# Peer lookup of a two-block layer: bank order of an output product, a choice cut in pieces, scores moved behind their queries

## The reference

```python
def peer(h, w_query, sub_keys, expert_down, expert_up):
    qry = (ht @ w_query).reshape(T, PEER_HEADS, 2, PEER_HALF)
    sub_scores = jnp.einsum('thpc,hpkc->thpk', qry, sub_keys)
    top_s, top_i = lax.top_k(sub_scores, K)
    cand_s = top_s[:, :, 0, :, None] + top_s[:, :, 1, None, :]
    cand_id = top_i[:, :, 0, :, None] * N_KEYS + top_i[:, :, 1, None, :]
    best_s, best_c = lax.top_k(cand_s.reshape(T, PEER_HEADS, K * K), K)
    expert_id = jnp.take_along_axis(cand_id..., best_c, axis=-1)
    gate = jax.nn.softmax(best_s, axis=-1)
    ...
        u = expert_down[ib]
        a = jnp.einsum('pd,ped->pe', xb, u)
        act = jax.nn.gelu(a, approximate=False) * gb
        v = expert_up[ib]
        return jnp.einsum('pe,ped->pd', act, v)
```

## Time and profile before

| | us |
|---|---|
| median of 3 runs | 1179.24 |
| lowest and highest run | 1175.29, 1180.07 |
| profiled execution | 1178.07 |
| its span | 1176.3 |
| PE busy | 1030.6 (88%) |
| DVE busy | 855.7 (73%) |
| ACT busy | 419.9 (36%) |
| POOL busy | 285.8 (24%) |
| DMA, mean over the span | 322 GB/s |
| mean granted clock of TensorE | 0.956 |

### The profile page before, as it was taken

How to read it: one execution, slowest core, us unless ns; L and a number is a source line. 1 busy time by engine, 2 the same in 40 slices (tenths; PEclk the granted TensorE clock), 3 DMA queues, 4 the chain that set the end, 5 groups by cost and what they waited for, 6 DMA issues and landing times.

```text
span 1176.3 us, 14387 instructions
## 1 busy us (share of the span) xinstructions
PE 1030.6 (88%) x5156; PEld 721.4 (61%) x5156; DVE 855.7 (73%) x1780; ACT 419.9 (36%) x833; POOL 285.8 (24%) x260
## 2 busy tenths in 40 slices
PE   6999999999999999988899998888668767887878
PEld 6988999999998876874555544333323323332433
DVE  5977689998868993384778767766786677677554
ACT  5644544445456654233223222221221222222112
POOL 0000000000000000034445543454335434443520
PEclk9999999999999999989999998898899889888998
DMA  9532449979927433479999999999999999999994
GB/s 357 204 125 90 147 180 350 354 293 322 326 89 309 139 109 124 180 284 340 364 420 422 422 421 421 422 420 421 423 422 421 422 422 419 423 421 421 422 421 183
DMA packets 67896, 378.61 MB, mean 322 GB/s; under 512 B 7537, under 2 KB 7921, under 8 KB 35057
## 3 DMA queue, kind: packets, MB, share of 16 engines
q0 software_dynamic: 36864, 268.45, 55.3%
q1 hardware_dynamic: 29808, 106.09, 25.0%
q10 hardware_dynamic: 1152, 3.15, 0.8%
HBM read 376.61 MB, written 1.05 MB: 321 GB/s over the span
## 4 chain that ended last, share of the span: by engine, by line
PE 45%; DMA 31%; DVE 15%; ACT 5%; issue 4%; POOL 1%; SPq 0%; DVEq 0%; ACTq 0%
DMA whi_rows<-in_peer,idsb 26%; PE pb L905 7%; PE pb L428 7%; PE pb L425 7%; PE pb L908 6%; PE pb L453 4%; DMA ring_sb<-in_peer,idsb 3%; DVE ring_lo L1417 3%; PE pb L640 2%; PE pb L810 2%; PE pb L860 1%; DVE ring_sb L2006 1%; PE pb L470 1%; PE pb L472 1%; PE pb L471 1%
## 5 line engine op out<-in xcount | busy, mean ns | idle before, releaser
L2006 DVE CUSTOM_DVE_ANT_0 ring_sb<-ring_sb,arena 128x1024 f32<-128x1024 f32 x137 | 166.9, 1225 | 106.8 <-DMA ring_sb<-in_peer,idsb 106.8
L905 PE MATMUL pb<-ring_sb,arena 128*128 128x512 f32 x274 | 154.2, 646 | 98.8 <-ACT arena L1358 98.7
L2062 POOL DMA_INDIRECT ring_sb<-in_peer,idsb x137 | 150.4, 1098 | 237.0 <-PE pb L908 210.2
L425 PE MATMUL pb<-xhi,whi 128*128 128x256 f32 x736 | 190.9, 293 | 1.1 <-ACT xhi L986 0.5
L428 PE MATMUL pb<-xlo,whi 128*128 128x256 f32 x736 | 186.3, 287 | 0.5 <-DVE xlo L1636 0.3
L2062 POOL DMA_INDIRECT arena<-in_peer,idsb x38 | 41.4, 1090 | 546.2 <-DVE idsb L1984 503.4
L1353 ACT ACTIVATE arena<-arena 128x4 f32<-128x4 f32 (+2 forms) x71 | 14.6, 205 | 400.4 <-DVE arena L2006 400.4
L1417 DVE TENSOR_TENSOR ring_lo<-ring_sb,whi 128x1024 fp32r<-128x1024 f32 x126 | 147.6, 1218 | 13.4 <-ACT whi L959 13.3
L905 PEld LDWEIGHTS pb<-ring_sb,arena 128*128 128x128 f32 x274 | 52.3, 202 | 167.9 <-issue 167.4
L908 PE MATMUL pb<-ring_sb,arena 128*128 128x512 f32 x274 | 151.0, 634 | 0.0
L425 PEld LDWEIGHTS pb<-xhi,whi 128*128 128x128 f32 x736 | 142.5, 194 | 5.4 <-issue 3.4
(11 more groups left out here) (356 smaller groups left out, 1783.8 us busy)
## 6 DMA issues: line engine op xcount, KB each, us to landing
ring_sb<-in_ada SPq DMA_DIRECT2D x48, 512.0 KB, 5.6
ring_sb<-in_w_gu SPq DMA_DIRECT2D x44, 512.0 KB, 6.9
ring_sb<-in_w_in SPq DMA_DIRECT2D x38, 512.0 KB, 8.3
ring_sb<-in_w_down SPq DMA_DIRECT2D x22, 512.0 KB, 5.9
ring_sb<-in_w_out SPq DMA_DIRECT2D x16, 512.0 KB, 3.6
ring_sb<-in_w_q SPq DMA_DIRECT2D x8, 512.0 KB, 3.6
whi_rows<-in_w_q SPq DMA_DIRECT2D x6, 512.0 KB, 7.5
ring_sb<-in_peer,idsb POOLq DMA_INDIRECT x137, 27.7
```

What stands on the lines that cost most here:

```text
L425: e.matmul(o, hi_w(u)[:, c], xh(k), start=start, stop=False, skip_group_check=skip)
L905: mm = e.matmul(pb[4 + 2 * tile][:, :], dgr[col % 8], o[:, 1024:1536], start=begin, stop=end)
L2006: e.tensor_tensor_reduce(o, o, h2t[tile], 1.0, 0.0, MUL, ADD, aa[:, col:col + 1]).then_inc(*VD.up(("dot", col)))
L2062: e.indirect_dma_start(rows_at[s], None, peer, bass.IndirectOffsetOnAxis(ap=idsb[:, col:col + 1], axis=0)).then_inc(s_row[s], 16)
```

## The change

1. The output product's four banks are taken one at a time, each just before its first use, in the order 0, 2, 3, 1 counted from the next in turn.
2. `experts` is cut into `best_of_list`, `pair_up`, `best_of_pairs` and `decode`, and `prepare` into `dot` and `weigh`. DVE's second choice (n = 1) stands in pieces between the dot products of rows 0 to 3. ACT's exponential of that choice moves behind group 1's scaled identities.
3. PE's query for tile 0 of head 2 moves behind the products of group 0; `second_sums` moves one group later. On ACT the root of tile 1's norm moves ahead of group 2's GELU.
4. The queries of heads 3 to 7 come one group earlier, and behind the products of that point instead of ahead of them; head 2's tile 1 moves from group 5 to group 9. Scores follow their queries by two groups, and ACT copies queries and scores one and three groups behind. Choice 3 moves from group 8 to 9, choices 4 to 15 one group later each.
5. POOL's table `after` counts from GR[i - 1]: buffers of heads 0 and 1 enter the list four rows later, head 2's twenty rows later, those of heads 3 to 7 behind the same row as before.

```diff
@@ -363,9 +363,9 @@
-        second_at = {3: 0, 4: 1, 5: 2}
-        query_at = {6: (3, 0), 7: (3, 1)} | {4 * h - 8 + j: (h, j) for h in range(4, 8) for j in range(2)}
-        choose_at = {4: 2, 8: 3} | {4 * n - 6: n for n in range(4, 16)}
+        second_at = {3: 0, 4: 1, 9: 2}
+        query_at = {5: (3, 0), 6: (3, 1)} | {4 * h - 9 + j: (h, j) for h in range(4, 8) for j in range(2)}
+        choose_at = {4: 2, 9: 3} | {4 * n - 5: n for n in range(4, 16)}
@@ -817,9 +817,10 @@
-            outs = [bank((VN, ("wo2", 2 * i + 1, 0))) for i in range(4)]
-            where["wo2"] = outs
+            outs = where["wo2"] = [(turn[0] + i) % 4 for i in (0, 2, 3, 1)]
+            turn[0] += 4
             for i in range(4):
+                bank((VN, ("wo2", 2 * i + 1, 0)), outs[i])
                 out_half(0, i, range(4, 8), pb[outs[i]])
             for i in range(4):
                 out_half(0, i, range(4), pb[outs[i]])
@@ -916,7 +917,6 @@
-            query_tile(2, 0)
@@ -926,21 +926,23 @@
             for i in range(NB + 1):
-                if i in second_at:
-                    query_tile(second_at[i], 1)
-                if i in query_at:
-                    query_half(*query_at[i])
                 if i == 60:
                     keep_clock(10)
                 if i:
                     add_rows(i - 1)
                 if i == 1:
+                    query_tile(2, 0)
+                if i == 2:
                     second_sums()
                     scores(2, (0,))
+                if i - 2 in second_at:
+                    scores(second_at[i - 2], (1,))
+                if i - 2 in query_at and query_at[i - 2][1]:
+                    scores(query_at[i - 2][0], (0, 1))
                 if i in second_at:
-                    scores(second_at[i], (1,))
-                if i in query_at and query_at[i][1]:
-                    scores(query_at[i][0], (0, 1))
+                    query_tile(second_at[i], 1)
+                if i in query_at:
+                    query_half(*query_at[i])
@@ -1320,15 +1322,17 @@
             def query_tile(h, tile):
                 e.wait_ge(*(USED.at(U_wq[2 * h + 1]) if tile else PQ.at(("qry", h))))
                 if h == 2:
-                    e.wait_ge(*PQ.at(("SC", 0, tile)))
+                    e.wait_ge(*PQ.at(("SC", 4) if tile else ("SC", 0, 0)))
...
             def query(h):
                 e.wait_ge(*USED.at(U_wq[2 * h + 1]))
-                e.wait_ge(*PQ.at(("SC", h - 2) if h >= 5 else ("SC", h - 2, 1)))
                 if h == 4:
                     e.wait_ge(*PQ.at(("SC", 2, 0)))
+                    e.wait_ge(*PQ.at(("SC", 0, 1)))
+                else:
+                    e.wait_ge(*PQ.at({3: ("SC", 1, 1), 5: ("SC", 3), 6: ("SC", 2, 1), 7: ("SC", 5)}[h]))
                 e.activation(qry[h % 2], pb[where["qry", h]][:, :], ACT.Copy).then_inc(*AQ.up(("qry", h)))
@@ -1370,27 +1374,28 @@
             choose(0)
             second_gate(range(4))
-            choose(1)
-            second_gate(range(4, 8))
             for i in range(NB + 1):
-                if i - 1 in query_at and query_at[i - 1][1]:
-                    scores(query_at[i - 1][0], (0, 1))
-                if i - 1 in second_at:
-                    scores(second_at[i - 1], (1,))
+                if i == 2:
+                    n3_root(1)
                 if i < NB:
                     prepare(i)
                 if i == 0:
+                    second_gate(range(4, 8))
+                if i == 1:
+                    choose(1)
                     query_tile(2, 0)
                     second_squares()
-                if i == 1:
-                    n3_root(1)
+                if i == 2:
                     scores(2, (0,))
-                if i == 2:
                     shifted(1)
-                if i in second_at:
-                    query_tile(second_at[i], 1)
-                if i in query_at and query_at[i][1]:
-                    query(query_at[i][0])
+                if i - 3 in second_at:
+                    scores(second_at[i - 3], (1,))
+                if i - 3 in query_at and query_at[i - 3][1]:
+                    scores(query_at[i - 3][0], (0, 1))
+                if i - 1 in second_at:
+                    query_tile(second_at[i - 1], 1)
+                if i - 1 in query_at and query_at[i - 1][1]:
+                    query(query_at[i - 1][0])
                 if i in choose_at:
                     choose(choose_at[i])
@@ -1923,32 +1928,44 @@
-            def experts(n):
+            def best_of_list(n, p):
...
+            def pair_up(n):
...
+            def best_of_pairs(n):
                 e.wait_ge(*VT.at((n, "cand")))
+                e.wait_ge(*AE.at(n - 1))
+                top16(cand, cand2, bsv, bcu[:, :], n, "best")
+                e.wait_ge(*VT.at((n, "best", "index2")))
+                e.tensor_scalar(nb, bsv[:, 0:1], -1.0, None, MUL).then_inc(*VT.up((n, "nb")))
+
+            def experts(n):
+                best_of_list(n, 0)
+                best_of_list(n, 1)
+                pair_up(n)
                 if n:
-                    e.wait_ge(*AE.at(n - 1))
-                    top16(cand, cand2, bsv, bcu[:, :], n, "best")
-                    e.wait_ge(*VT.at((n, "best", "index2")))
-                    e.tensor_scalar(nb, bsv[:, 0:1], -1.0, None, MUL).then_inc(*VT.up((n, "nb")))
+                    best_of_pairs(n)
                     decode(n, 0, 16)
                     return
@@ -1994,21 +2011,26 @@
+            def dot(col):
...
+            def weigh(i):
...
+            def prepare(i):
+                for col in GR[i]:
+                    dot(col)
+                weigh(i)
@@ -2027,12 +2049,22 @@
             choose(0)
-            choose(1)
-            for i in range(NB + 1):
+            best_of_list(1, 0)
+            dot(0)
+            best_of_list(1, 1)
+            dot(1)
+            pair_up(1)
+            weigh(0)
+            best_of_pairs(1)
+            dot(2)
+            dot(3)
+            decode(1, 0, 16)
+            weigh(1)
+            second_add()
+            gates(1)
+            for i in range(2, NB + 1):
                 if i < NB:
                     prepare(i)
-                if i == 0:
-                    second_add()
                 if i == 2:
                     second_norm()
@@ -2047,7 +2079,7 @@
-            after = {GR[i - 2][-1]: h for i, h in second_at.items()} | {GR[i - 2][-1]: h for i, (h, j) in query_at.items() if j}
+            after = {GR[i - 1][-1]: h for i, h in second_at.items()} | {GR[i - 1][-1]: h for i, (h, j) in query_at.items() if j}
```

More of the change, by code:

```diff
@@ L1924, in top16 @@
                 e.max_index(idx[:, 8:16], vals[:, 8:16], tmp_).then_inc(*VT.up((*name, "index2")))
-            def experts(n):
+            def best_of_list(n, p):
                 tile, h = n // 8, n % 8
-                if n == 0:
-                    e.wait_ge(*PQ.at(("SC", 0, 0)))
-                elif tile == 0:
-                    e.wait_ge(*AQ.at(("SC", h) if h >= 3 else ("SC", h, 0)))
-                if n:
-                    e.wait_ge(*VT.at((n - 1, "gates")))
-                    e.wait_ge(*VTI.at(n - 1))
-                for p in range(2):
-                    s = SC[tile][:, (2 * h + p) * 128:(2 * h + p + 1) * 128] if n else pb[where["SC", h, 0]][:, p * 128:(p + 1) * 128]
-                    if p:
-                        e.wait_ge(*VT.at((n, 0, "index2")))
-                    top16(s, sc2[:, 0:128], tsv[:, p * 16:p * 16 + 16], tiu[:, p * 16:p * 16 + 16], n, p)
+                if p == 0:
+                    if n == 0:
+                        e.wait_ge(*PQ.at(("SC", 0, 0)))
+                    elif tile == 0:
+                        e.wait_ge(*AQ.at(("SC", h) if h >= 3 else ("SC", h, 0)))
+                    if n:
+                        e.wait_ge(*VT.at((n - 1, "gates")))
+                        e.wait_ge(*VTI.at(n - 1))
+                s = SC[tile][:, (2 * h + p) * 128:(2 * h + p + 1) * 128] if n else pb[where["SC", h, 0]][:, p * 128:(p + 1) * 128]
+                if p:
+                    e.wait_ge(*VT.at((n, 0, "index2")))
+                top16(s, sc2[:, 0:128], tsv[:, p * 16:p * 16 + 16], tiu[:, p * 16:p * 16 + 16], n, p)
+            def pair_up(n):
                 e.wait_ge(*VT.at((n, 1, "index2")))
@@ L1995, in choose @@
                 gates(n)
-            def prepare(i):
-                for col in GR[i]:
-                    tile = col // 128
-                    s, v = row_of[col]
-                    o = rows_at[s][:, 0:1024]
-                    e.wait_ge(s_row[s], v)
-                    if col % 128 == 0:
-                        for g in range(2):
-                            e.wait_ge(*AQ.at((("h2t", tile), g)))
-                    e.tensor_tensor_reduce(o, o, h2t[tile], 1.0, 0.0, MUL, ADD,
-                                           aa[:, col:col + 1]).then_inc(*VD.up(("dot", col)))
+            def dot(col):
+                tile = col // 128
+                s, v = row_of[col]
```

(7 more changed lines are left out.)

1 line of the change is left out of this document (added).

## The result

| | before | after |
|---|---|---|
| median | 1178.90 us (4 runs) | 1169.49 us (4 runs) |
| lowest and highest | 1175.29, 1180.07 | 1169.03, 1170.56 |
| span of the profiled execution | 1176.3 | 1167.2 |
| first gather issued | 503.82 | 498.73 |

The medians lie 9.4 us apart, where 9.6 were forecast. The ratio of the means is 0.9927, 95% interval 0.9904 to 0.9949, thus 8.6 us (6.0 to 11.3). The total is right within the noise; the account under it is not, and the rest of this document is about that.

What follows compares the result with a forecast made beforehand. The gathers' DMA queue bounds the kernel, so only DMA time lost before 600 us counts: 2.3 us from an earlier first gather plus 7.3 from holes make 9.6, 1179.2 - 9.6 = 1169.6 us, range 1164.5 to 1177.0.

Steps and rivals of the forecast that it cites:

- The bound: Software DMA queue: gathers run at 420 GB/s after 600 us, so the end moves by DMA time lost before.
- The banks: Output product: PE's 2.27 us wait for L1875 goes, first gather at 501.5, 2.3 us gained.
- The second choice in pieces: DVE, rows 0 to 3: PE starts row 0 at about 512.3 instead of 520.39; gather 7's hole closes.
- What is late next: Gather 11, taking row 4's buffer behind the second norm's root: hole 2.8 us plus 0.8 slow restart, 3.6 us.
- a lump of 1.3: Allowance for slow PE rows at a lower clock behind gaps at 510-512 and 526-530: 1.3 us, bounds 0 and 3.
- Scores two groups behind: Third choice: row 16 through at 566.4, no hole by 1.3 us, so the 3.6 us lost in 580-600 go.
- The sum: Lost after the first issue 7.7 instead of 15.0 us, gain 7.3, with 2.3 in front 9.6: 1169.6 us.
- The signs: Refuted by first gather still at 503.8, a hole behind gather 24, or a clock under 0.8 in 510-560.
- Everything hides: Group 2 comes in time and the clock stays up, only 2.8 us remain lost: 1164.7 us, chance 0.13.
- Only the start counts: Holes before 600 us stay as large as now, gain 2.3 us: 1176.9 us, chance 0.14.
- Loads twice as dear: ACT's root chain: its two table loads cost 2.6 us more: 1172.2 us, chance 0.05.
- PE as the bound at a low clock: Groups 2 to 8: at low clock each group loses 11 us; 1185 to 1190 us, chance 0.06.

Runs made afterwards that it cites:

- the table of two by two: Second choice whole or in pieces, with old or new queries and return, all with new banks: 1174.38, 1175.39, 1176.53, and 1169.49 and 1169.79 us.
- the last kernel: Changed kernel with the root behind group 2, matmuls in PE's gaps before rows 4 and 12, and the third choice one group earlier: 1164.86 us.

## Why the prediction was right, and where it was not

**The bound.** Right in the main: between 600 us and the last gathers no kernel but the one with the old return lost more than 0.4 us, and the times follow roughly what the gathers lost before. In the table of two by two, 15.8, 18.1, 18.0 and 12.5 (mean of two) lost go with 1174.4, 1175.4, 1176.5 and 1169.6. The stretch behind the last gather varies by up to 2.6 us, which the prediction left out.

**The banks.** The mechanism was right, the size a little small: 2.3 forecast, 2.7 by matched profiles, 2.4 to 4.1 by the medians. The product's second half did not wait for the gated vectors.

**The second choice in pieces.** Its walk held. Counted from the first gather, row 0 stood on PE at 11.4 us (forecast 10.8) and dot product 4 on DVE at 21.2 (20.8); DVE waited 1.34 us for the exponential (1.5). Gather 7 came at 15.0 instead of 12.9, as row 0 stood 0.6 later and ran at the low clock, and still without a hole.

**What is late next.** The hole was named at the right place and undersized: 3.6 forecast for gathers 11 and 12, 7.4 lost at 11 to 14 in the first profile and 4.6 in the second. GELU came at 28.9 us behind the first gather and not 27.7: the sums of squares stood behind rows 2 and 3 in PE's own order, with second_add done at 518.3 and ACT's squares at 520.8, where the prediction had them wait for those two alone. The rest is the low clock behind the gap of 3.87 us, which I had only as a lump of 1.3. With the gap filled, 3.9 is lost there. The text also says that the root now stands ahead of group 2's GELU; it stood there before as well (the GELU follows the load at 530.97 in the old trace). What is new is that gather 11 hangs on row 4.

**Scores two groups behind.** This step failed. "No hole by 1.3 us" came out as a hole of 3.0 us at gathers 25 to 27, in both profiles. Rows 12 to 15 landed later since gather 11 was late, and DVE waited for each of them (1.55, 2.76, 1.95 and 1.25 us), the last as

```profile
550.72 1.23 DVE L2022 CUSTOM_DVE_ANT_0 ring_sb<-ring_sb,arena 128x1024 f32<-128x1024 f32 x1 [1.25 <-DMA ring_sb<-in_peer,idsb]
```

The third choice stands behind these dot products, and so row 16 stood on PE 68.8 us behind the first gather (66.4 in the second profile) instead of 63.2, and then ran at the low clock. In the last kernel, with the choice a group earlier and the gaps filled, these gathers lost 0.8 together. A slip of 0.3 in the working doesn't matter beside this: 542.7 to 566.4 is 23.7 us and not 24.0. The hole at gather 26 was moved, not removed: 3.6 before, 3.0 after.

**The sum.** Of the 9.6 us, 7.3 were for the holes. Counted as the prediction counts (the first gather's latency of 1.8 us, and what is lost up to 600 us), the kernel before lost 15.6 and 16.0 us in its two profiles and the changed one 13.7 and 11.7, where 7.7 was forecast: 3.1 us won in the mean. By the medians it is 3.5 to 5.3 over the banks alone. So the term for the holes was 2 to 4 us too large. What made up for it in the first measurement is not a gain that the prediction had: the banks' median is larger than their wait, and the profile had the luck of two absent low stretches ahead of its first gather and of a short end. How much of the medians' 9.4 is such chance stays open; measured again the change was worth 7.7. That the median fell within 0.2 us of the forecast is luck. I had also priced the pieces and the queries as two terms of a sum; neither kernel that lacks one of them beat the banks alone, though the third part stood in both.

**The signs.** The prediction named signs that would make it wrong, and one came: a hole behind gather 24. Nor did every stretch from 540 us on run at 420 GB/s (405, 355, 413). The closed hole at gather 7, POOL's wait for gather 11 until 532.6 and the scores near 560 came as forecast; the first gather came 2.8 us earlier than forecast in one profile of the changed kernel and 1.4 in the other, so that the wait until 532.6 is longer than it seems.

**The rivals.** Everything hides: no, the low clock and the root remain. Only the start counts: no, though the kernels without the pieces or without the queries' part did no better than that. Loads twice as dear: no, see ACT's rows above. PE as the bound at a low clock: not seen; the lowest clock between 500 and 600 us is 0.83 over 20 us, and PE keeps up with the gathers behind it.

## What to carry to other kernels

With a fixed ring of buffers, a buffer's return is one link in a list: follow the next two or three buffers in turn behind the one you speed up, for they decide whether its gain stays. Price edits on the same ring together and test them two by two, with every other part of the change the same in all four kernels. When an engine runs dry ahead of the work that returns buffers, add the slow rows behind the gap to the price, or fill the gap.

## What was not expected of the hardware

The low stretches of TensorE's clock are partly chance and partly gaps. Ahead of 461 us PE waits some 1.13 and 0.79 us in every kernel, as here in the second profile of the changed one, which did not lose its clock:

```profile
459.36 0.65 PE L678 MATMUL pb<-arena 128*64 128x256 f32 x4 [1.13 <-DVE arena L1853]
459.81 0.42 PE L680 MATMUL pb<-arena 128*64 128x128 f32 x4
461.02 1.10 PE L779 MATMUL pb<-xn,cs 128*128 128x512 f32 x2 [0.79 <-ACT xn L1262]
```

In six profiles a low stretch stood at 460.6 to 461.4, and each of them had one at 54.4 to 55.2 as well; in the three with one at 55.3 to 55.8, and in the five with none near 55, there was none near 461. Without the banks' wait the output product began at 470.2 to 470.7 with these stretches and at 467.8 to 469.4 without the one at 461, so an execution's luck there is up to 2.9 us, more than the wait that the change removed. Behind the gap of 3.87 us ahead of row 4 the clock fell in both profiles of the changed kernel and in the one of all but the banks (3.88), and not where matmuls filled it. Ahead of row 16 it isn't so sure: behind a gap of 3.53 or 3.54 us it fell in both profiles of the changed kernel, in that of the root behind group 2 and in that with matmuls ahead of row 4 alone, but not in that of all but the banks. The Trainium skill, TensorE: Matmul & The Clock Gate, What's actually happening, says that idleness throttles and activity releases; row 4 with and without the matmuls agrees. What decides whether a given wait brings the clock down stays open.

A gather behind an idle queue is followed by a slow one: behind the hole at gather 11 gather 12 lost 0.7 to 0.8 us in all fourteen profiles.
